# Output projection of the mixing: token block by token block, with each block normalized on its own

## The reference, cut to what matters

```python
# 256 tokens of width 1024; two layers of this block, then two layers of another one (not touched)
for l in range(2):
    mix = token_mixing(x, ...)                       # ends in: merged @ w_out[l]   (1024 x 1024)
    x   = layer_norm(DN_ALPHA * x + mix, ln1_g[l], ln1_b[l])
    ffn = moe(x, w_router, router_bias, w1[l], w3[l], w2[l])   # 16 experts, the best 2 of each token
    x   = layer_norm(DN_ALPHA * x + ffn, ln2_g[l], ln2_b[l])

def layer_norm(x, g, b):
    mu  = mean(x);  var = mean((x - mu)**2)
    return (x - mu) * rsqrt(var + 1e-5) * g + b

def moe(x2, ...):
    scores = sigmoid(x2 @ w_router)                  # all tokens are needed before slots are given out
    ...                                              # best group, best two experts, a slot for each token
    h = silu(xb @ w1[e]) * (xb @ w3[e]);  y = h @ w2[e]
```

## Time and profile before

| what | us |
|---|---|
| median of 3 runs (lowest, highest) | 1908.03 (1907.16, 1909.44) |
| the profiled execution: its own time | 1908.67 |
| its span in the trace | 1907.2 |
| TensorE busy in the span | 1690.6 (89%) |
| VectorE busy, ScalarE busy | 858.1 (45%), 709.3 (37%) |
| weights' queue (q1), share of 16 DMA engines' span | 52.2% |
| mean granted TensorE clock | 0.933 of full speed |

### The profile page before, as it was taken

How to read it: one execution, slowest core, us unless ns; L and a number is a source line. 1 busy time by engine, 2 the same in 40 slices (tenths; PEclk the granted TensorE clock), 3 DMA queues, 4 the chain that set the end, 5 groups by cost and what they waited for, 6 DMA issues and landing times. The chain is left out here.

```text
span 1907.2 us, 23163 instructions
## 1 busy us (share of the span) xinstructions
PE 1690.6 (89%) x9672; PEld 1296.7 (68%) x9672; DVE 858.1 (45%) x1564; ACT 709.3 (37%) x1091; POOL 29.1 (2%) x49
## 2 busy tenths in 40 slices
PE   6899998998978998998998978768999987689998
PEld 5788996433336788996443337646899776468997
DVE  6466565110116575564111027454655464545554
ACT  4356542111113347541111124632544346325442
POOL 4000000000000000000000000000000000000000
PEclk9999999999998999999999989757999997579999
DMA  9343445999984342465999964202455442014552
GB/s 301 121 140 111 157 177 218 400 421 421 422 328 154 136 148 98 155 230 202 422 421 421 422 261 159 88 1 73 170 179 197 144 166 89 1 66 156 198 178 109
DMA packets 57557, 393.88 MB, mean 207 GB/s; under 512 B 7140, under 2 KB 7184, under 8 KB 15200
## 3 DMA queue, kind: packets, MB, share of 16 engines
q1 hardware_dynamic: 54288, 381.35, 52.2%
q0 software_dynamic: 3008, 9.61, 1.7%
q10 hardware_dynamic: 144, 1.30, 0.2%
HBM read 391.18 MB, written 1.05 MB: 206 GB/s over the span
## 5 line engine op out<-in xcount | busy, mean ns | idle before, releaser
L1547 DVE TENSOR_TENSOR ring_rounded<-ring_sb,ring_rounded 128x2048 fp32r<-128x2048 f32 (+4 forms) x180 | 385.6, 2155 | 245.2 <-ACT ring_rounded L1178 245.0
L1178 ACT ACTIVATE ring_rounded<-ring_sb 128x2048 fp32r<-128x2048 f32 (+4 forms) x180 | 322.1, 1803 | 206.6 <-PE psum L562 174.9
L562 PE MATMUL psum<-ring_sb,region_sb 128*64 128x512 f32 x1536 | 345.7, 601 | 34.9 <-DMA ring_sb<-in_weights 22.3
L562 PE MATMUL psum<-xT_hi_rounded,ring_rounded 128*128 128x256 f32 x1920 | 352.4, 285 | 0.0
L562 PEld LDWEIGHTS psum<-xT_hi_rounded,ring_rounded 128*128 128x128 f32 x1920 | 302.5, 194 | 0.6
L562 PE MATMUL psum<-ring_rounded,region_rounded 128*128 128x512 f32 x1184 | 290.7, 397 | 6.0 <-DVE memory_kv_rounded L2191 3.0
L562 PEld LDWEIGHTS psum<-ring_sb,region_sb 128*64 128x64 f32 x1536 | 113.0, 138 | 248.5 <-issue 231.3
L562 PE MATMUL psum<-xT_lo_rounded,ring_rounded 128*128 128x256 f32 x960 | 276.3, 288 | 5.8 <-DVE xT_lo_rounded L1977 5.8
L562 PEld LDWEIGHTS psum<-ring_rounded,region_rounded 128*128 128x128 f32 x1184 | 225.2, 191 | 55.4 <-issue 3.8
L562 PE MATMUL psum<-ring_rounded,xT_hi_rounded 128*128 128x384 f32 (+4 forms) x832 | 237.4, 363 | 20.3 <-DVE ring_rounded L1547 11.9
L562 PEld LDWEIGHTS psum<-xT_lo_rounded,ring_rounded 128*128 128x128 f32 x960 | 185.9, 194 | 8.7 <-DVE xT_lo_rounded L1977 6.2
(11 more groups left out here) (261 smaller groups left out, 1474.3 us busy)
## 6 DMA issues: line engine op xcount, KB each, us to landing
ring_sb<-in_weights SPq DMA_DIRECT2D x324, 1024.0 KB, 9.4
ring_sb<-in_weights SPq DMA_DIRECT2D x24, 768.0 KB, 4.4
ring_sb<-in_weights SPq DMA_DIRECT2D x8, 904.0 KB, 4.5
ring_sb<-in_weights SPq DMA_DIRECT2D x8, 900.0 KB, 4.5
ring_sb<-in_weights SPq DMA_DIRECT2D x8, 584.0 KB, 11.4
region_sb<-in_mem_turned POOLq DMA_DIRECT2D x2, 1024.0 KB, 7.4
region_sb<-in_pool_band POOLq DMA_DIRECT2D x2, 1024.0 KB, 9.4
region_sb<-in_ln_g POOLq DMA_DIRECT2D x4, 512.0 KB, 4.2
```

What stands on the lines that cost most here:

```text
L562: return nc.tensor.matmul(dst, lhsT, rhs, start=first, stop=last, skip_group_check=True)
L1178: nc.scalar.activation(rounded(piece.hi), piece.raw, ACT.Copy).then_inc(hi_made, 1)
L1547: nc.vector.tensor_tensor(rounded(piece.raw), piece.raw, reread(piece.hi), ALU.subtract).then_inc(lo_made, 1)
```

## The change

The projection of the first block's mixing gets its own function, in which all four pieces are taken first and the loop over token blocks is the outer one: block 0 with pieces 38, 39, 40, 41, then block 1 with the same four. The slots of each piece are released in block 1. The normalization of the mixing gets its own function too, in which a block is added, measured, combined and normalized before the next is begun; ScalarE makes the root of each block in an instruction of its own. The normalization after the experts is the same instructions as before, in a function of its own; only the numbers on the semaphores differ.

```diff
+        def pe_held_by_block(l, name, lhs, ready):
+            pieces = [[ring.next() for _ in range(2)] for _ in range(2)]
+            for b in range(TB):
+                for half in range(2):
+                    _, free, full = dense.take((name, l, half, b), x_added.at(l, b * 2 + half), at=b * 2 + half)
+                    pe.wait_ge(*free)
+                    for part_, piece in enumerate(pieces[half]):
+                        pe_wait_weights(piece)
+                        for c in range(KC // 2):
+                            k = part_ * KC // 2 + c
+                            pe.wait_ge(*ready[k // 2])
+                            last = product(held[:, b, half * BANK:(half + 1) * BANK],
+                                           [o[:, k, b * P:(b + 1) * P] for o in lhs], [w[:, c, :] for w in parts(piece)],
+                                           k == 0, k == KC - 1)
+                        if part_:
+                            last.then_inc(full, 1)
+                            if b == TB - 1:
+                                ring.release(piece, dense.of((name, l, half, b))[1])
+                        elif b == TB - 1:
+                            used(last, piece)
...
-            pe_held(l, "mixed", [merged_upper, mergedT], [merged_lo.at(l, c) for c in range(4)])
+            pe_held_by_block(l, "mixed", [merged_upper, mergedT], [merged_lo.at(l, c) for c in range(4)])
...
         def act_norm(l, phase):
             moments, root = stat("ln_moments", TB, 2), stat("ln_root", TB)
-            a.wait_ge(*ln_aggregated.at(l, phase))
-            nc.scalar.activation(root, moments[:, :, 1], ACT.Sqrt, bias=const("ln_eps")).then_inc(ln_rooted.sem, 1)
+            for n, blocks in enumerate([slice(0, TB)] if phase else [slice(b, b + 1) for b in range(TB)]):
+                a.wait_ge(*ln_aggregated.at(l, 2 * phase + n))
+                nc.scalar.activation(root[:, blocks], moments[:, blocks, 1], ACT.Sqrt, bias=const("ln_eps")).then_inc(ln_rooted.sem, 1)
...
+        def vec_norm_mixed(l):
+            stats_, moments, root = stat("ln_stats", TB, 2, 6), stat("ln_moments", TB, 2), stat("ln_root", TB)
+            for b in range(TB):
+                for half in range(2):
+                    cols = slice(half * BANK, (half + 1) * BANK)
+                    v.wait_ge(*dense.of(("mixed", l, half, b))[1])
+                    v.wait_ge(x_in, 32)
+                    nc.vector.scalar_tensor_tensor(x[:, b, cols], x[:, b, cols], DN_ALPHA, held[:, b, cols], ALU.mult,
+                                                   ALU.add).then_inc(x_added.sem, 1)
+                    v.wait_ge(*x_added.at(l, b * 2 + half))
+                    nc.vector.bn_stats(stats_[:, b, half, :], x[:, b, cols]).then_inc(*vs.next())
+                vs.settle()
+                nc.vector.bn_aggr(moments[:, b, :], stats_[:, b, :, :].rearrange("p k s -> p (k s)")).then_inc(ln_aggregated.sem, 1)
+                v.wait_ge(*ln_aggregated.at(l, b))
+                v.wait_ge(norm_in.sem, 32 * (2 * l + 1))
+                nc.vector.scalar_tensor_tensor(x[:, b, :], x[:, b, :], moments[:, b, 0:1], norm_rows[:, 0, :], ALU.subtract,
+                                               ALU.mult).then_inc(*vs.next())
+                v.wait_ge(*ln_rooted.at(l, b))
+                nc.vector.reciprocal(root[:, b:b + 1], root[:, b:b + 1]).then_inc(*vs.next())
+                vs.settle()
+                nc.vector.scalar_tensor_tensor(x[:, b, :], x[:, b, :], root[:, b:b + 1], norm_rows[:, 1, :], ALU.mult,
+                                               ALU.add).then_inc(x_normed.sem, 1)
...
             round_lo(first + 42)
-            vec_norm(l, 0)
+            vec_norm_mixed(l)
```

More of the change, by code:

```diff
@@ L493, in build_program @@
         xT_hi, xT_lo, x_normed, x_added = (signal(n, c) for n, c in (("xT_hi", 8), ("xT_lo", 8), ("x_normed", 4), ("x_added", 6)))
-        ln_aggregated, ln_rooted = signal("ln_aggregated", 2), signal("ln_rooted", 2)
+        ln_aggregated, ln_rooted = signal("ln_aggregated", 3), signal("ln_rooted", 3)
         z_made = signal("z_made", 2 * len(Z_CUTS))
@@ L673, in pe_held @@
                         if part_ == 0:
-                            _, free, full = dense.take(key, x_added.at(l, half * 2 + b) if name == "mixed" else res_added.at(l, half * 2 + b),
-                                                       at=b * 2 + half)
+                            _, free, full = dense.take(key, res_added.at(l, half * 2 + b), at=b * 2 + half)
                             pe.wait_ge(*free)
@@ L1631, in vec_merge, with vec_norm_experts @@
                 nc.vector.tensor_tensor(mergedT[:, dc, :], mergedT[:, dc, :], gate, ALU.add).then_inc(merged.sem, 1)
[L1633 removed]
+        def vec_norm_mixed(l):
[20 more added lines that the diff above has]
+                                               ALU.add).then_inc(x_normed.sem, 1)
+        def vec_norm_experts(l, ahead):
             stats_, moments, root = stat("ln_stats", TB, 2, 6), stat("ln_moments", TB, 2), stat("ln_root", TB)
@@ L1638, in vec_norm @@
                 for b in range(TB):
-                    _, full = dense.of((("mixed", "experts")[phase], l, half, b))
-                    v.wait_ge(*full)
-                    if phase == 0:
-                        v.wait_ge(x_in, 32)
-                        nc.vector.scalar_tensor_tensor(x[:, b, cols], x[:, b, cols], DN_ALPHA, held[:, b, cols], ALU.mult,
-                                                       ALU.add).then_inc(x_added.sem, 1)
-                        v.wait_ge(*x_added.at(l, half * 2 + b))
-                    nc.vector.bn_stats(stats_[:, b, half, :], (held if phase else x)[:, b, cols]).then_inc(*vs.next())
+                    v.wait_ge(*dense.of(("experts", l, half, b))[1])
+                    nc.vector.bn_stats(stats_[:, b, half, :], held[:, b, cols]).then_inc(*vs.next())
             vs.settle()
@@ L1651, in vec_norm @@
             vs.settle()
-            v.wait_ge(*ln_aggregated.at(l, phase))
-            v.wait_ge(norm_in.sem, 32 * (2 * l + phase + 1))
+            v.wait_ge(*ln_aggregated.at(l, 2))
+            v.wait_ge(norm_in.sem, 32 * (2 * l + 2))
             for b in range(TB):
-                nc.vector.scalar_tensor_tensor(x[:, b, :], (held if phase else x)[:, b, :], moments[:, b, 0:1], norm_rows[:, 0, :],
-                                               ALU.subtract, ALU.mult).then_inc(*((x_added.sem, 1) if phase else vs.next()))
+                nc.vector.scalar_tensor_tensor(x[:, b, :], held[:, b, :], moments[:, b, 0:1], norm_rows[:, 0, :], ALU.subtract,
+                                               ALU.mult).then_inc(x_added.sem, 1)
                 if b == 0:
-                    v.wait_ge(*ln_rooted.at(l, phase))
+                    v.wait_ge(*ln_rooted.at(l, 2))
                     nc.vector.reciprocal(root, root).then_inc(*vs.next())
                 vs.settle()
-                if phase:
-                    v.wait_ge(*x_added.at(l, 4 + b))
+                v.wait_ge(*x_added.at(l, 4 + b))
                 nc.vector.scalar_tensor_tensor(x[:, b, :], x[:, b, :], root[:, b:b + 1], norm_rows[:, 1, :], ALU.mult,
@@ L2428, in build_program @@
                     late_tokens(l)
-            vec_norm(l, 1, ring_first[l + 1] + 1)
+            vec_norm_experts(l, ring_first[l + 1] + 1)
             round_hi(ring_first[l + 1] + 1)
```

1 line of the change is left out of this document (removed).

## The result

Forecast were 1905.2 us, a gain of 2.8. Measured were 1910.35 us (median of 20 runs, 1905.81 to 1914.49) against 1905.30 for the kernel before in the same comparison (20 runs, 1898.33 to 1911.21): ratio 1.0027, interval 1.0017 to 1.0038. Two more comparisons of the same two kernels gave 1.0012 [0.9994, 1.0030] and 1.0022 [1.0007, 1.0037]. All three point to a cost of 0.1 to 0.3%, some 2 to 5 us. The gain of 2.8 us, a ratio of 0.9985, lies outside all three intervals. The base of the forecast, 1908.03 from three runs, was itself 2.7 above the median of 20. The profile of e7 is of a disturbed execution with a lower clock throughout (0.825 on average), so its stages are not read; all other profiles and all ratios are of undisturbed ones.

The account below looks back on a forecast made before the run. The bound was taken as dependent steps from projection to first expert matmul, delaying the weight stream. Savings of 1.36 (layer 0) and 1.43 us (layer 1), together 2.8, against the 1908.03 median gave 1905.2 us; range 1903.1 to 1907.4.

Parts of the forecast that it names:

- Order of the products: Projection on TensorE: new waits for split pieces before units 3 and 4, together 1.12 us in layer 0, 0.96 in layer 1.
- VectorE's queue, ScalarE's root: Block 0's normalization fits between 293.5 and 298 us beside block 1's products; the second root hides behind a 1.28 us pass.
- sign 2: In the changed profile, block 0's second normalization pass is over near 298 us.
- After E: From TensorE's end of projection (E): router at E + 7.57 in layer 0; 2.48 us saved there, 2.39 in layer 1.
- The sum to the restart: Saving behind the projection less its new waits, before the weight stream restarts: 1.36 us in layer 0, 1.43 in layer 1.
- Slots of the ring: Weight slots released later in the projection; 9.4 MB refill ends about 318 to 326 us, hidden by the standstill, cost nothing.
- sign 5: Transfer rate at zero for a few us before the experts' first issue, near 333.4 us.
- the only one on the slower side: Ring fills too late for the expert stage: 6.4 us late a layer, 1920.8 us; chance 0.03.
- the rival with the nearest number: In the expert stages, longer waits for weights swallow the earlier stream start: no change, 1908.0 us; chance 0.11.
- From the router on all steps follow each other as before: Everything behind the router keeps its sequence, so the 2.8 us saved in both layers reaches the end.
- I leave the sum: Sum kept at 2.8 us despite possible clock shifts (0.7 to 4.9); the 2.3 us spread of runs stands for them.
- the clock: Granted clock 1.00 from 245 to 326 us; two later episodes, at 559 and 1123, could each change, differing by 1.07 us.

Follow-up runs that it names:

- e7: The changed kernel with one VectorE instruction less in each layer's expert stage (ScalarE copies half of the slots' gates); 1906.16 us, ratio 1.0004.
- e9: The changed kernel with the slots' gates' 32 small matmuls spread over pair 1's first weights; 1917.05 us (7 runs), ratio 1.0075.
- e1: The changed kernel again, no edit, for a second profile; 1908.79 us.
- e5: The kernel before again, no edit, timed against itself; 1909.59 us, ratio 1.0022.
- e6: The kernel before with one tiny unused VectorE copy more in layer 0's expert stage; 1905.24 us, ratio 0.9999.
- e16: The kernel before with one tiny unused VectorE copy more, the same edit as e6 a second time; 1906.43 us, ratio 1.0001.
- e12: The changed kernel a third time, no edit; 1908.73 us.
- e13: The changed kernel with one VectorE instruction less a layer, the same edit as e7 a second time; 1906.08 us, ratio 0.9996.
- e15: The changed kernel with one tiny unused VectorE copy more in layer 0's expert stage; 1908.02 us, ratio 1.0001.
- e2: The changed kernel with 10 in place of 5 filler products before the first gather of tokens; 1913.63 us, ratio 1.0039.
- e14: The kernel before with only TensorE's order changed, block by block, and the old normalization; 1911.86 us, ratio 1.0028.

## Why the prediction was wrong, step by step

*Order of the products: right in the sum.* Forecast were waits of 0.46 and 0.66 us, in layer 1 0.46 and 0.50. By the pitch of 2.774 units 3 and 4 started 0.55 and 0.41 late (287.54 - 281.44 - 5.55; 290.72 - 287.54 - 2.77), in layer 1 the same; the idle time in the rows, 0.39 and 0.17, is less, since the end of a matmul before a wait is modelled later. Over the whole projection it is 304.70 - 281.44 = 23.26 against 22.19: 1.07 more for 1.12 forecast, in layer 1 1.05 for 0.96.

*VectorE's queue, ScalarE's root: right.* Block 0's second pass was over at 298.17 (sign 2).

*After E: right to 0.2.* Router at E + 7.39 for E + 7.57, in layer 1 E + 7.30. Block 1's subtracting pass started at E + 1.89, as forecast; the 0.18 that I had added for the copies of block 0 on ScalarE and VectorE didn't show, and without it the sum is 4.63 + 2.76 = 7.39. The router stood at 312.09 (forecast 312.2). For layer 1 the forecast was 873.8 and the trace has 877.55: the stages between, not the step, are off by 3.7.

*The sum to the restart: right.* 1.36 and 1.43 forecast, 1.4 to 1.7 measured in all profiles.

*Slots of the ring: right.* The refill ran at 427 and 416 GB/s and was over by 324, and no byte moved from 324 to 326 (sign 5). That rival, the only one on the slower side, had no part in the result. Nor had the rival with the nearest number, the stream that swallows an earlier start (1908.0): in e9 the earlier start arrives at N through the same dip of the stream.

*The step that failed* is the one that cost everything behind the router at nothing: "From the router on all steps follow each other as before", together with "I leave the sum" under the clock. They don't follow as before. The profile of before shows a clock at 1.00 over the small products at 345 and over the mixing at 656, and I took this as a property of that work. It was one of its place. Work 1.4 us earlier got the lower clock for the first, and one VectorE instruction more helped to get it for the second. I had weighed the clock for the two episodes that the trace of before showed (the one at 559 went from 8.41 to 8.55, in e1 to 9.11), and bounded it by 1.07 each. That bound fails for the kernel before itself, in whose second profile, e5, the same 32 matmuls take 10.09:

```profile
559.86 10.09 PE L562 MATMUL psum<-ring_sb,region_sb 128*64 128x512 f32 x32 [0.69 <-ACT region_sb L1409]
```

The spread of three runs, 2.3 us, which was to stand for the clock, is 12.9 over 20 runs of the same kernel. And what counted most were episodes that the trace of before doesn't contain. The mis-sized term is thus the clock's: taken at nothing in the sum, with about 2 us in either direction as its bound; the two stages in which it shows came out 1.4 (layer 0's experts) and 3.9 us longer (layer 1's mixing), 5.3 together against 3.1 won.

The Trainium skill (TensorE: Matmul & The Clock Gate, Part 1, What's actually happening) says that the activity window "doesn't reset when your kernel starts" and that the point of the change so differs between runs. For the point within the work the trace agrees: what the clock does hangs on where work stands against it. The next fall of the layer begins 220.2 us after the restart in both profiles of the kernel before and 221.5 to 221.8 after it in all three of the kernel after. Counted from F it is 508.6 in all five: this fall stayed where it was, and the work moved against it. The small products start at F + 298.6 in before, e5, e6 and e16, without a fall, and at F + 296.9 to 297.3 in after, e1, e12, e13 and e15 (and e2), where a fall begins at F + 300.4 each time; in e14 they start at F + 300.7, and it begins at F + 303.8. For the difference between runs the trace agrees in part: much of it is fixed once F is, but before and e5 leave the same place, F + 288.4, and take 236.65 and 238.41. To let the spread of repeated runs stand for the clock, as I did, overlooked that a shift of the work moves it the same way in every run.

**What stays open.** What took the gain in layer 0's expert stage is argued: the fall beside the small products fits it there and doesn't in layer 1. Of layer 1's mixing, 2.5 to 3.3 us go with the late start (after and e12 against before, e1 against e13 and e15, each at the same place against F). What the place alone does, 271.5 to 274.1 us, no run set by itself: it is read from profiles that came to stand there, and a longer expert stage ahead of it is what puts N later. Why the clock falls behind small products at one place and not 1.4 us later, the runs don't say. Nor is it shown why VectorE's stream has a place at which an instruction issues late. No version here is faster than both kernels: e13 is level with the kernel before.

## What to carry to other kernels

In a kernel bound by TensorE a gain of 1 to 2 us in one stretch has to be followed through every later stage, for each stretch of small products or short waits may meet the clock otherwise once it is shifted (here the falls at 347 and 657 us); a clock of 1.00 in the trace of before says only that it held at that place. Compare stage lengths between two or three profiles of each kernel before believing a difference of 0.2% either way, and time the kernel before against itself once. Every added instruction, a 0.16 us reciprocal too, moves all behind it in its engine's stream: try the same change with the count restored.

## What the runs showed of the hardware that was not expected

- TensorE counted as busy for 3.00 of 3.00 us with products of 16 columns (344 to 347 us of the kernel after), and still had the clock halved from 346.8 to 350.3. It kept the clock when they stood 1.4 us later (before), and when they were spread between products of 512 columns (e9).
- An instruction of VectorE whose inputs were there started 0.30 us later than usual (0.44 us behind the start of the one ahead of it in place of 0.14, shown as 0.21 to 0.22 us idle) in each of nine profiles in which exactly one more instruction stood ahead of it, and in none of the eight with none or two more.
- The granted clock repeats: two executions of the kernel after on different occasions (after and e12) have their falls, from layer 0's restart to layer 1's projection, at the same distances to 0.1 us, and the two stages took 238.07 and 238.19, 275.61 and 275.63. In layer 1's experts they part, and the third execution, e1, parts from them behind the small products already: its fall there lasts 7 us where theirs last 3.
